# Gating scale and bias on VectorE, and the second block's softmax normalisation ahead of the third block's maxima

## The reference

```python
h = x @ w_in + b_in
c = silu(layer_norm(causal_depthwise_conv(a * sigmoid(g), conv_w, conv_b), ...))   # 256 channels
att = sliding_window_sink_attention(q, k, v, sinks)                                # 8 heads of 64
z = gelu(h[..., OFF_GMLP:])                                                        # 512 channels
v = layer_norm(z[..., 256:], ln_g, ln_b)
gm = z[..., :256] * (einsum('hij,bsjhc->bsihc', where(mask, w_s, 0), v) + b_s)
out = concatenate([c, att, gm]) @ w_out + b_out
```

## Time and profile before

| what | us |
|---|---|
| median of three runs | 943.93 |
| lowest and highest run | 942.88, 945.69 |
| the profiled execution, its own time | 938.3 |
| its span, first to last instruction | 936.5 |
| TensorE busy in the span | 867.4 (93%) |
| VectorE busy | 403.8 (43%) |
| ScalarE busy | 253.6 (27%) |
| GpSimd busy | 300.3 (32%) |

### The profile page before, as it was taken

One profiled execution on the slowest core, in us unless ns is written; L12 is line 12 of the kernel. 1 busy time (PEld: TensorE's weight loads), 2 busy tenths in 40 slices (PEclk: granted clock), 3 DMA queues, 4 the chain that ended last, 5 costly groups with the idle time before them and its releaser, 6 DMA issues.

```text
span 936.5 us, 15865 instructions
## 1 busy us (share of the span) xinstructions
PE 867.4 (93%) x5987; PEld 570.8 (61%) x5987; DVE 403.8 (43%) x924; ACT 253.6 (27%) x473; POOL 300.3 (32%) x223
## 2 busy tenths in 40 slices
PE   6999799889999998999999997998899999979995
PEld 5877578755555554555488776787555555545551
DVE  5997746732111111111559977467321111111126
ACT  5324842301111111111233248423012111111111
POOL 0632446222222221221534324462222222212233
PEclk9999899979999999999999998999799999999998
DMA  9761067799999999996814210677999999999955
GB/s 322 279 226 56 11 266 308 283 416 405 404 407 401 408 406 406 403 396 196 178 38 135 91 55 9 265 311 293 416 399 346 400 406 405 408 408 399 401 146 163
DMA packets 66278, 273.33 MB, mean 292 GB/s; under 512 B 8722, under 2 KB 24242, under 8 KB 41136
## 3 DMA queue, kind: packets, MB, share of 16 engines
q1 hardware_dynamic: 53792, 247.14, 66.1%
q0 software_dynamic: 12432, 25.41, 11.2%
HBM read 256.83 MB, written 22.02 MB: 298 GB/s over the span
## 4 chain that ended last, share of the span: by engine, by line
PE 65%; DVE 20%; DMA 10%; issue 2%; ACT 2%; POOL 0%; DVEq 0%; SPq 0%; ACTq 0%; POOLq 0%
PE bank L790 28%; PE bank L445 15%; PE bank L796 14%; DMA w_down<-in_exp_w_down 8%; DVE bank L1168 8%; PE bank L773 2%; DVE xTl L1137 2%; DMA moemem<-x_rows,first_tok 2%; DVE w_gate L1144 1%; PE bank L780 1%; PE bank L840 1%; PE bank L783 1%; DVE w_gate L1145 1%; DVE w_down L1143 1%; DVE xtok L1299 1%
## 5 line engine op out<-in xcount | busy, mean ns | idle before, releaser
L1414 DVE TENSOR_TENSOR moemem<-bank,moemem 64x128 f32<-64x128 f32 x172 | 48.3, 281 | 309.1 <-ACT moemem L1046 306.4
L1634 POOL DMA_INDIRECT moemem<-x_rows,gather_idx x43 | 44.9, 1045 | 284.5 <-DVE moemem L1428 260.4
L790 PE MATMUL bank<-w_up,moemem 128*64 128x256 f32 x1088 | 126.5, 386 | 2.2 <-DMA w_up<-in_exp_w_wide 2.2
L1581 POOL TENSOR_TENSOR wl<-w_gate,wh 128x2048 fp32r<-128x2048 f32 x17 | 78.0, 4590 | 126.4 <-ACT wh L909 98.4
L445 PE MATMUL bank<-xTh,wh 128*128 128x512 f32 (+1 forms) x256 | 101.1, 395 | 11.2 <-DVE xTl L1137 9.9
L790 PEld LDWEIGHTS bank<-w_up,moemem 128*64 128x64 f32 x1088 | 79.6, 140 | 47.1 <-issue 10.6
L1046 ACT ACTIVATE moemem<-bank 64x256 f32<-64x256 f32 x86 | 32.7, 381 | 246.3 <-PE bank L790 246.3
L445 PE MATMUL bank<-xTl,wh 128*128 128x512 f32 (+1 forms) x256 | 95.4, 373 | 0.0
L445 PE MATMUL bank<-xTh,wl 128*128 128x512 f32 (+1 forms) x256 | 95.2, 372 | 0.0
L1628 POOL DMA_INDIRECT y_rows<-moemem,scatter_idx x44 | 71.0, 1614 | 62.3 <-ACT moemem L1051 54.5
L790 PE MATMUL bank<-w_gate,moemem 128*64 128x256 f32 x736 | 83.4, 379 | 3.7 <-DMA w_gate<-in_exp_w_wide 3.7
(11 more groups left out here) (227 smaller groups left out, 1278.9 us busy)
## 6 DMA issues: line engine op xcount, KB each, us to landing
w_up<-in_exp_w_wide SPq DMA_DIRECT2D x24, 2048.0 KB
w_gate<-in_exp_w_wide SPq DMA_DIRECT2D x16, 2048.0 KB, 20.6
w_down<-in_exp_w_down SPq DMA_DIRECT2D x16, 2048.0 KB, 25.1
w_down<-in_exp_w_wide SPq DMA_DIRECT2D x8, 2048.0 KB
w_gate<-in_exp_w_down SPq DMA_DIRECT2D x8, 2048.0 KB
xtok<-in_exp_w_wide SPq DMA_DIRECT2D x8, 2048.0 KB, 24.4
moex<-in_exp_w_wide SPq DMA_DIRECT2D x8, 2048.0 KB
moew<-in_exp_w_down SPq DMA_DIRECT2D x8, 2048.0 KB
```

Of the source, the lines that this page charges most:

```text
L790: return [pe.matmul(bank[i][CH * n:CH * n + CH, 0:256], x, w[:, 512 * n + 256 * i:512 * n + 256 * i + 256], start=(k == 0), stop=(k == KD ...
L1414: dve.tensor_tensor(he[CH * b:CH * b + CH, P * i:P * i + P], bank[i][0:CH, P * b:P * b + P], silu[:, 256 * i + P * b:256 * i + P * b + P], ...
L1581: pool.tensor_tensor(wl[(n + l) % SLOTS][:, :], wraw[n % 2], wh[(n + l) % SLOTS][:, :].bitcast(F32), ALU.subtract)\
L1634: return pool.indirect_dma_start(to, None, x1_halves[l], bass.IndirectOffsetOnAxis(ap=rows[:, :], axis=0), bounds_check=2 * T - 1, oob_is_ ...
```

## The change

GpSimd no longer touches the gating values. VectorE's first pass takes the scale instead of rstd and no longer waits for the power; it waits for the scale and bias rows instead, and signals `gvh_set` as before. A second pass of four instructions on VectorE multiplies by rstd and adds the bias, and signals `gvn_set`; it stands behind the maxima of block 2 and waits for the power there. The normalisation of block 1 stands ahead of the maxima of block 2.

```diff
@@ VectorE @@
                    .then_inc(diag_set, 1)
-                dve.wait_ge(grstd_set, l + 1)
-                for j in range(TT):
-                    link(dve.tensor_scalar(gv[:, j, :], gsrc[j], mv[:, 2 * j:2 * j + 1], rstd[:, j:j + 1],
-                                           ALU.subtract, ALU.mult))
+                dve.wait_ge(row_in, 16 * (l + 1))
+                for j in range(TT):
+                    link(dve.scalar_tensor_tensor(gv[:, j, :], gsrc[j], mv[:, 2 * j:2 * j + 1], rowm[:, 0:GM],
+                                                  ALU.subtract, ALU.mult))
                 dve.sem_inc(gvh_set, 1)
                 dve.wait_ge(spread_done, l + 1)
                 dve.wait_ge(cen_set, 2 * (l + 1))
                 for m in range(2):
                     dve.tensor_tensor(cv[:, m, :], cv[:, m, :], bank[7][:, :], ALU.mult).then_inc(conv_norm, 1)
+                softmax_norm(l, 1)
                 softmax_max(l, 2)
-                softmax_norm(l, 1)
+                dve.wait_ge(grstd_set, l + 1)
+                for j in range(TT):
+                    link(dve.scalar_tensor_tensor(gv[:, j, :], gv[:, j, :], rstd[:, j:j + 1], rowm[:, GM:2 * GM],
+                                                  ALU.mult, ALU.add))
+                dve.sem_inc(gvn_set, 1)
                 heads_low(l, 0)
                 copy_turned(l, 1)
                 conv_lows(l)
@@ GpSimd @@
                 pool.wait_ge(gvar_set, l + 1)
                 pool.tensor_tensor(rstd, ve, mhalf, ALU.pow).then_inc(grstd_set, 1)
 
-                pool.wait_ge(gvh_set, l + 1)
-                pool.wait_ge(row_in, 16 * (l + 1))
-                for i, op in ((0, ALU.mult), (1, ALU.add)):
-                    link(pool.tensor_tensor(gv, gv, rowm[:, GM * i:GM * i + GM].unsqueeze(1).broadcast_to([P, TT, GM]), op))
-                pool.sem_inc(gvn_set, 1)
                 pool.wait_ge(pn_done, TT * l + 2)
                 piece_lows(l, 8)
                 piece_lows(l, 9)
```

## The result

The changed kernel takes 951.76 us (median of 15 runs, 946.28 to 955.53), the kernel before 945.66 in the same series. The ratio is 1.0070, 95% interval 1.0049 to 1.0091, which is 6.6 us slower (4.6 to 8.6); it is estimated from the fast runs, without two executions of the kernel before that took 1786.83 and 2962.59 us, and so it is not the quotient of the two medians (1.0065). The forecast was slower by 4.5 us, 948.4, in a range that ended at 951.5. So the sign was right and the size too small; the median lies just outside the range, also because the kernel before came out 1.7 us above the 943.93 that the sum was added to. The profiled execution took 946.28 us with a span of 944.2, against 938.3 and 936.5 before. It is the fastest of the 15, as the profiled execution of the kernel before was faster than any timed one (the lowest of all series is 940.21).

A forecast was written before the change was run, and what follows sets the result against it. The chain was 65% TensorE and 20% VectorE, with TensorE's transposes waiting for VectorE's normalisation. Delays of 1.1 and 2.7 us plus 2 x 0.35 of clock made 4.5 us, added to 943.9: 948.4 us, range 943.9 to 951.5.

The forecast's parts named there:

- The mechanism: Third block's maxima: L1189, with SBUF operands, waits from 107.2 to 110.47 until GpSimd's earlier-released subtraction ends.
- Rival 1: At L1189 the wait does not come or costs little: gain of 2.4 us, 941.5; chance 0.10.
- The first pass: VectorE's gating pass with the scale: four instructions of about 0.5 us, some 2.1 us.
- The gain of 0.2 us ahead of L1509: Layer 0: the conv multiply starts at 103.0 instead of 103.20, limited by TensorE's spread.
- The second pass: VectorE behind the third block's maxima: at most 2.9 us, more likely 2, in idle time, so cost 0.
- The conv subtractions: On VectorE ahead of the third block's normalisation: they meet no GpSimd and take 2 x 0.6 instead of 2.67 us.
- 1.1 us late: Layer 0: the third block's normalisation on VectorE starts at 116.77 instead of 115.68.
- Layer 1: TensorE's transposes of the third block (L612) come at 588.4 instead of 585.69, 2.7 us late.
- 0 to 1.0 us a layer, I take 0.35: Low TensorE clock behind the longer idle stretch, in attend and the transposes: 0.35 us taken for each layer.
- rival 3: Low clock lasts over the transposes into the output projection in both layers: +6.5 us, 950.4; chance 0.09.
- Passed on in full: Behind the stretch TensorE is busy 19.58 of 21 us, so the whole delay reaches the end; bound 0.3 to 1.
- rival 2: Delay partly absorbed later in waits for expert weights: +1.5 to +2.5 us, 945.9; chance 0.13.

The follow-up runs named there:

- z4: The kernel before, unchanged, run once more: 945.4 us, span 943.6.
- z1: The changed kernel with 15 unused TensorE products between the second block's transposes and the fourth block's scores: 947.56 us, ratio 1.0038 to the kernel before.
- x1: The changed kernel with GpSimd's piece 8 subtraction started behind VectorE's second gating pass, not the second block's normalisation: 947.38 us, ratio 1.0022.
- y2: The changed kernel with VectorE's old order: third block's maxima, second gating pass, then second block's normalisation: 946.43 us, ratio 1.0014.
- z3: The changed kernel, order kept, with GpSimd's piece 8 subtraction released as soon as its high part is there: 944.18 us, ratio 1.0012.
- x3: The kernel before with only the order changed (second block's normalisation ahead of third block's maxima), GpSimd keeping the gating: 955.73 us, ratio 1.0124.
- x2: The changed kernel with the third block's maxima first again and GpSimd's piece 8 subtraction released once its high part is there: 942.55 us, ratio 0.9983.
- z2: x2 with 6 unused TensorE products ahead of the second block's transposes: 939.72 us, ratio 0.9950 to the kernel before.
- x4: The kernel before with 12 small unused VectorE instructions (2.4 us a layer) ahead of the third block's normalisation: 954.94 us, ratio 1.0123.

## Why the forecast was right in sign and too small

L1509 to the third block's L612, then L1509 of layer 0 to the end of the span, in us, with the ratio of the whole kernel:

| kernel | layer 0 | layer 1 | to the end | ratio |
|---|---|---|---|---|
| before, first profile | 14.2 | 12.8 | 833.3 | 1 |
| before, z4 | 12.3 | 12.8 | 833.7 | 1 |
| changed | 16.2 | 15.9 | 840.7 | 1.0070 |
| changed, filled (z1) | 15.5 | 15.5 | 841.0 | 1.0038 |
| x1, subtraction late | 14.3 | 14.3 | 836.6 | 1.0022 |
| y2, gating alone | 14.5 | 14.5 | 836.6 | 1.0014 |
| z3, subtraction early | 14.0 | 12.9 | 836.9 | 1.0012 |
| x3, order alone | 19.3 | 17.1 | 847.5 | 1.0124 |
| x2, early, maxima first | 11.3 | 11.2 | 832.9 | 0.9983 |
| z2, the same, filled | 11.2 | 11.2 | 830.2 | 0.9950 |

Point by point.

- **The mechanism** was right. L1189 takes 3.25 and 3.24 us and ends 0.03 us behind GpSimd's instruction; I had it waiting from 107.2 to 110.47, it did from 107.75 to 111.00. Moving that instruction elsewhere (x1, z3) takes two thirds of the cost away or all of it that can be measured. The rest of L1189's delay is the order, which my sum also held (it has L1189 arrive at 107.2 where it had arrived at 105.85). Rival 1 (no wait, 941.5) is out: the page of the Trainium skill that speaks of a shared interface and contention (GPSIMD Engine Reference, "Key points") has to be read here as all or nothing, since an instruction of eight columns waited for the rest of one of 2048.
- **The first pass**: right. L1503 takes 2.03 us for four where I took 2.1. The gain of 0.2 us ahead of L1509 did not show: it started at 103.53, behind TensorE, and not at 103.0.
- **The second pass** costs nothing: 2.04 us in idle time, as forecast.
- **The conv subtractions** run free (1.28 us), as forecast.
- **Layer 0, "1.1 us late"**, is the step that failed: the term was mis-sized. It was a difference to an execution in which L1189 had already lost 1.9 us to GpSimd. Against that same execution it is 1.3 (z1, without the low clock, 15.5 against 14.2), near the forecast. In z4 L1189 loses nothing there, and against z4 the changed kernel's VectorE path is 3.2 us late (15.5 against 12.3). Layer 1 is 2.7 us late against either, as forecast (15.5 against 12.8). How often an execution is of the one kind or the other the timed runs don't show. Of the five profiles with the old code three are like z4; z4's 945.4 us lies near the median, and none of the timed executions was as fast as the 938.3 of the first. So the term lies between 1.3 and 3.2, more likely near the upper end.
- **The clock, "0 to 1.0 us a layer, I take 0.35"**: it cost 0.7 and 0.4 us in the stretches (16.2 against 15.5, 15.9 against 15.5), 0.4 more in all than I took. Whether it costs anything behind them, as rival 3 had it, isn't shown: in the changed kernel's profile the third block's transposes run at full clock (1.09 us) in both layers.
- **Passed on in full**: right. Outside the two stretches, from L1509 of layer 0 to the end, the changed kernel has 808.6 us and z4 808.7; the first profile has 806.3. So rival 2 (absorbed) has nothing for it here, and against z4 nothing is enlarged either. x4 cost more than one to one, but its pause lies ahead of the output projection's products.
- **Two readings of rows** were slightly off, without effect on the sum: the clock came back at 115.3 and not 115.2 (a mean of 0.67 over 115.0 to 115.5 in the earlier trace rows), and of the waits called four long ones in the rows, the one at 575.56 is short (0.66 us in all).

Put together, against z4: 3.2 and 2.7 us on VectorE's path and 0.7 and 0.4 of clock make 7.0 us, where the timed runs show 6.6 (4.6 to 8.6). Against the first profile the same terms make 5.1. The sum of 4.5 lies just under that interval, and another 1.7 us of the miss in the absolute time is the kernel before, which came out higher than in the three runs that I had. That 7.0 comes so near to 6.6 is in part luck, since each side is a single execution.

The choice behind the error was one. The profiled execution took 938.3 us against a median of 943.9, and I had noted the 5.6 us between them and added my sum on top without asking what differed. Between it and z4, 6.6 of the 7.1 us in span lie ahead of L1509 of layer 0 (103.20 against 109.84), where the clock was low in z4, and with that came a difference in which instructions met each other.

## What to carry to other kernels

When an instruction is moved, follow every semaphore that it gives: here the gain was on TensorE, and the loss came from a GpSimd instruction that the same signal released, onto an eight-column VectorE instruction with both operands in SBUF. In this kernel the long GpSimd instruction did best beside VectorE work that reads PSUM. When a fix brings a kernel back to the old time, compare the versions with each other too: z3 looked as if the order were free, and x2 showed that it was not. And before a sum is made of a single execution, look whether it is a usual one: a profile that is faster than every timed run can have other waits than they have, as the 2.07 us of L1189 against z4's 0.17 show.

## What the runs showed of the hardware that I had not expected

A pause of TensorE ahead of the output projection cost more than its length: 2.4 us a layer cost 11.6 us in all (x4, 8.5 to 14.6). Unused products in an idle stretch made two kernels faster, by 3.0 us (z1 against the changed kernel, about 0.3 to 5.8) and 3.1 us (z2 against x2, about 0.5 to 5.7); both pairs are from different series. A product of 128x256 with plain float32 operands, here as the fill, is recorded as two and takes 0.44 us at full clock (11.39 us for 52 records). And a VectorE instruction with a scalar column and two SBUF operands, L1514, takes the same 0.51 us at 256 columns as the first pass (L1503) with one operand in PSUM (2.04 and 2.03 for four).
